# Loading the input in four quarters and spreading its transposes over the first three steps of a 1-core transformer kernel

## What is computed

```python
def rmsnorm(x, g, eps=NORM_EPS):
    xf = x.astype(jnp.float32)
    y = xf * lax.rsqrt(jnp.mean(xf * xf, axis=-1, keepdims=True) + eps)
    return (y * g.astype(jnp.float32)).astype(x.dtype)

for l in range(DEPTH):                 # DEPTH = 2
    h = rmsnorm(x, norm_g[l])
    proj = h @ w_in[l]                 # (256 x 1024) @ (1024 x 4096)
    ...                                # attention on parts of proj, gates
    x = x + y @ w_out[l]
```

## Time and profile before

| what | value |
|---|---|
| runs | 1212.27, 1209.83, 1209.98 us; median 1209.98 |
| the profiled execution's own time | 1208.38 us |
| its span | 1206.5 us |
| PE busy | 1187.9 us (98%) |
| DVE busy | 800.3 us (66%) |
| ACT busy | 586.7 us (49%) |
| POOL busy | 556.9 us (46%) |
| loaded | 297.92 MB, 247 GB/s in the mean |
| mean granted clock of PE | 0.999 |

### The profile page before, as it was taken

How to read it: one execution, slowest core, us unless ns; L and a number is a source line. 1 busy time by engine, 2 the same in 40 slices (tenths; PEclk the granted TensorE clock), 3 DMA queues, 4 the chain that set the end, 5 groups by cost and what they waited for, 6 DMA issues and landing times.

```text
span 1206.5 us, 15432 instructions
## 1 busy us (share of the span) xinstructions
PE 1187.9 (98%) x5752; PEld 975.4 (81%) x5752; DVE 800.3 (66%) x1118; ACT 586.7 (49%) x764; POOL 556.9 (46%) x418
## 2 busy tenths in 40 slices
PE   9999999999899999899999999999999999999998
PEld 6888887887688888788888888888888887888887
DVE  6885468844687688578768666697683675644423
ACT  5566465665543443444434357444352665534440
POOL 1466334564544343555454226764452462445460
PEclk9999999999999999999999999999999999999999
DMA  9976369845698899549988748799884444866550
GB/s 355 356 273 227 108 244 333 287 146 184 215 344 287 304 337 349 168 155 339 302 301 315 279 174 273 250 327 303 303 297 165 150 154 157 261 211 208 209 193 35
DMA packets 183224, 297.92 MB, mean 247 GB/s; under 512 B 8368, under 2 KB 100208, under 8 KB 183152
## 3 DMA queue, kind: packets, MB, share of 16 engines
q1 hardware_dynamic: 177696, 284.82, 68.2%
q10 hardware_dynamic: 5456, 12.13, 2.9%
HBM read 295.84 MB, written 1.08 MB: 246 GB/s over the span
## 4 chain that ended last, share of the span: by engine, by line
PE 88%; DVE 5%; POOL 2%; ACT 2%; issue 1%; SPq 1%; DMA 1%; ACTq 0%; DVEq 0%
PE ps L1821 26%; PE ps L1834 26%; PE ps L1826 25%; PE ps L2087 2%; PE ps L1848 1%; POOL w_lo L510 1%; PE ps L1971 1%; PE ps L1913 1%; PE ps L1999 1%; ACT w_hi L640 1%; DVE w_lo L1157 1%; PE ps L1987 1%; DMA raw<-w_in 1%; SPq L468 1%; PE ps L1959 1%
## 5 line engine op out<-in xcount | busy, mean ns | idle before, releaser
L510 POOL TENSOR_TENSOR w_lo<-raw,w_hi 128x512 fp32r<-128x512 f32 x348 | 479.5, 1411 | 447.0 <-ACT w_hi L640 447.0
L640 ACT ACTIVATE w_hi<-raw 128x2048 fp32r<-128x2048 f32 x188 | 354.6, 1910 | 102.9 <-PE ps L1834 68.8
L1821 PE MATMUL ps<-w_hi,h_hi 128*128 128x512 f32 x1120 | 313.8, 402 | 1.0 <-issue 1.0
L1834 PE MATMUL ps<-w_lo,h_hi 128*128 128x512 f32 x1120 | 301.4, 391 | 2.7 <-POOL w_lo L521 0.8
L1826 PE MATMUL ps<-w_hi,h_lo 128*128 128x512 f32 x1120 | 300.6, 390 | 0.0
L1157 DVE TENSOR_TENSOR w_lo<-raw,w_hi 128x2048 fp32r<-128x2048 f32 x96 | 224.9, 2346 | 111.4 <-ACT w_hi L640 108.6
L1834 PEld LDWEIGHTS ps<-w_lo,h_hi 128*128 128x128 f32 x1120 | 209.3, 188 | 50.1 <-issue 2.1
L1826 PEld LDWEIGHTS ps<-w_hi,h_lo 128*128 128x128 f32 x1120 | 210.1, 188 | 46.2 <-DVE h_lo L1218 0.2
L1821 PEld LDWEIGHTS ps<-w_hi,h_hi 128*128 128x128 f32 x1120 | 200.6, 188 | 43.7 <-issue 6.9
L1143 DVE SCALAR_TENSOR_TENSOR ps<-ada_raw,ccol,ps 128x512 f32<-128x512 f32 x240 | 181.0, 754 | 8.7 <-DMA ada_raw<-ada_w 2.0
L913 ACT ACTIVATE a_hi<-ps 128x512 fp32r<-128x512 f32 x44 | 26.3, 599 | 160.6 <-PE ps L2087 160.6
(11 more groups left out here) (198 smaller groups left out, 981.2 us busy)
## 6 DMA issues: line engine op xcount, KB each, us to landing
raw<-ffn_in SPq DMA_DIRECT2D x176, 512.0 KB, 5.7
ada_raw<-ada_w SPq DMA_DIRECT2D x144, 512.0 KB, 7.2
raw<-ffn_out SPq DMA_DIRECT2D x44, 1024.0 KB, 6.5
raw<-w_in SPq DMA_DIRECT2D x31, 1024.0 KB, 8.6
raw<-w_out SPq DMA_DIRECT2D x8, 1024.0 KB, 6.4
ada_raw<-kv_ada_w SPq DMA_DIRECT2D x16, 512.0 KB, 8.5
raw<-w_kv SPq DMA_DIRECT2D x8, 1024.0 KB, 6.0
bias<-na_bias ACTq DMA_DIRECT2D x16, 256.0 KB, 4.2
```

Source lines behind the costliest of these rows:

```text
L510: ins = pool.tensor_tensor(w_lo[:, u % RAW, piece], raw[:, u % RAW, piece], w_hi[:, u % RING, piece].bitcast(F32), ALU.subtract)
L640: act.activation(w_hi[:, u % RING, :], raw[:, u % RAW, :], ACT.Copy).then_inc(*S.inc("w_hi_ready", u))
L1821: pe.matmul(bank(b), hi[:, k_in_lhs + k, tok], wh[:, k, c * 512:(c + 1) * 512], start=start and k == 0, stop=False)
L1834: ins = pe.matmul(bank(b), hi[:, k_in_lhs + k, tok], wl[:, k, c * 512:(c + 1) * 512], start=False, stop=stop and k == nk - 1)
```

## The change

x is loaded in four quarters (token block by column half, 256 KB each), each with a semaphore of its own. On SP the order is x(0,0), first half of unit 0, x(1,0), second half of unit 0, x(0,1), x(1,1), unit 1. PE does two `warm_up` matmuls at the start instead of three, turns x(0,0) alone, and turns the other three quarters one by one in the middle of steps 0, 1 and 2: x(1,0), x(0,1), x(1,1). In the steps of unit 0 the matmuls on `w_hi` go by halves of the unit: `h_hi` and `h_lo` with its first two row blocks, then both with the other two. On ACT, `w_hi` of unit 1 stands between the `h_hi` of x(0,1) and that of x(1,1). DVE's order is the same as before.

```diff
-WARM_UP = (3, 1)
+WARM_UP = (2, 1)
...
-            sp.dma_start(x[:, 0, :], x_in[0:P, :]).then_inc(x_in_sem[0], 16)
+            def load_x(t, half):
+                cols = slice(512 * half, 512 * half + 512)
+                sp.dma_start(x[:, t, cols], x_in[t * P:(t + 1) * P, cols]).then_inc(x_in_sem[t][half], 16)
+
+            load_x(0, 0)
...
                             raw_in[0] if k else half_in, 16)
+                        if k == 0:
+                            load_x(1, 0)
...
                 if u == 0:
-                    sp.dma_start(x[:, 1, :], x_in[P:2 * P, :]).then_inc(x_in_sem[1], 16)
+                    load_x(0, 1)
+                    load_x(1, 1)
...
                 for t in range(NT):
+                    if t:
+                        fill(1)
                     act.wait_ge(*S.at("xT_done", "a0", t, 1))
...
                     ins.then_inc(*S.inc("h_hi_ready", "a0", t, 1))
-                fill(1)
                 act.wait_ge(*S.at("stat_filled"))
...
-                for k in range(nk):
-                    if u == 0 and k == nk // 2:
+                for part in (range(0, nk // 2), range(nk // 2, nk)) if u == 0 else (range(nk),):
+                    if u == 0 and part[0]:
                         pe.wait_ge(*S.at("w_hi_ready", 0))
-                    for c, b in enumerate(banks):
-                        pe.matmul(bank(b), hi[:, k_in_lhs + k, tok], wh[:, k, c * 512:(c + 1) * 512],
-                                  start=start and k == 0, stop=False)
-                lhs_wait(lo_ready)
-                for k in range(nk):
-                    for c, b in enumerate(banks):
-                        pe.matmul(bank(b), lo[:, k_in_lhs + k, tok], wh[:, k, c * 512:(c + 1) * 512],
-                                  start=False, stop=False)
+                    for k in part:
+                        for c, b in enumerate(banks):
+                            pe.matmul(bank(b), hi[:, k_in_lhs + k, tok], wh[:, k, c * 512:(c + 1) * 512],
+                                      start=start and k == 0, stop=False)
+                    lhs_wait(lo_ready)
+                    for k in part:
+                        for c, b in enumerate(banks):
+                            pe.matmul(bank(b), lo[:, k_in_lhs + k, tok], wh[:, k, c * 512:(c + 1) * 512],
+                                      start=False, stop=False)
                 between()
...
+            def raw_T(t, half):
+                pe.wait_ge(x_in_sem[t][half], 16)
+                transpose_half("a0", t, half, "xT_done")
...
                 if layer == 0:
-                    norm_T(name, 0)
+                    raw_T(0, 0)
                     warm_up(WARM_UP[1])
...
                 def between(s):
-                    if s == 0 and not layer:
-                        norm_T(name, 1)
+                    if s < 3 and not layer:
+                        raw_T(*((1, 0), (0, 1), (1, 1))[s])
```

More of the change, by code:

```diff
@@ L335, in program @@
         bias_in = [ctx.enter_context(nc.semaphore(f"bias_in{i}")) for i in range(BIASES)]
-        x_in_sem = [ctx.enter_context(nc.semaphore(f"x_loaded{t}")) for t in range(NT)]
+        x_in_sem = [[ctx.enter_context(nc.semaphore(f"x_loaded{t}_{half}")) for half in range(2)] for t in range(NT)]
         ROWS = {("down", 0, 0): 2, "pool": 5, "pool_scale": 4, "pool_shift": 3, ("down", 0, 1): 8,
@@ L806, in first_norm @@
                     ins.then_inc(*S.inc("h_hi_ready", "a0", t, 1))
-                fill(1)
                 act.wait_ge(*S.at("stat_filled"))
                 for t in range(NT):
-                    act.wait_ge(x_in_sem[t], 16)
+                    for half in range(2):
+                        act.wait_ge(x_in_sem[t][half], 16)
                     act.activation(hn[:, t, :], x[:, t, :], ACT.Square, accum_out=st(t)).then_inc(
@@ L1916, in norm_T @@
             def norm_T(name, t, hat=None):
-                if name == "a0":
-                    pe.wait_ge(x_in_sem[t], 16)
                 for half in range(2):
-                    transpose_half(name, t, half, "xT_done", [("x_hat_ready", hat or name, t)] if name != "a0" else ())
+                    transpose_half(name, t, half, "xT_done", [("x_hat_ready", hat or name, t)])
+            def raw_T(t, half):
+                pe.wait_ge(x_in_sem[t][half], 16)
+                transpose_half("a0", t, half, "xT_done")
             def mix_part(half, to, of):
```

## The result

| | before | after |
|---|---|---|
| median of the runs | 1210.99 us (4 runs, 1209.83 to 1212.27) | 1221.16 us (4 runs, 1220.42 to 1224.92) |
| ratio, 95% interval | | 1.009 [1.0065, 1.0114] |
| the profiled execution: time, span | 1208.38, 1206.5 us | 1224.92, 1222.8 us |
| its mean granted clock | 0.999 | 0.991 |

The changed kernel is slower by 0.9%, 10.2 us. The forecast was 1218.4 us, a loss of 8.4. The profiled execution of the changed kernel is the slowest of its four (the others took 1220.4 to 1221.4 us, at a clock of 0.994 to 0.996), so its trace shows more loss than the median: its span is 16.3 us longer than that of the kernel before.

A forecast was written before the change was run, and what follows sets the result against it. PE's own list was taken to set the end (busy 1187.9 of 1206.5 us). Stalls 7.2 - 0.2 given back + 1.4 for the clock = 8.4 us, on 1210.0 giving 1218.4 us; range 1214.5 to 1221.5 us.

The forecast's parts named there:

- The mechanism: Step 2: PE waits 2.1 us for ACT's `w_hi` of unit 1, then 4.7 us for DVE's `w_lo` of unit 1.
- Rival C: Step 2: only the first wait comes, as DVE makes `w_lo` of unit 1 ahead of x(1,1); 1212.1 us, chance 0.03.
- rival D: Not slower: loads go on during the stalls and PE catches up; 1210.0 or 1209.1 us, chance 0.05.
- rival A: Both waits of step 2 come but the clock stays high; loss 7.0 us, 1217.0 us, chance 0.18.
- rival B: Later PE waits, up to 300 us, swallow part of the loss; 4.8 to 6.2 us left, about 1215.5 us, chance 0.09.
- the clock: one fall, for 1.4 us: Step 2: PE comes out of the 4.7 us wait at 1.2 GHz, losing 1.4 us, the middle of 0 and 2.65.
- bound of 2.65 us: Upper bound of the clock loss behind step 2's second wait, from some 5.3 us of half-pace work at the start.
- the 7.2 us of the stalls: Step 2's `w_lo` matmuls start at 24.5 us instead of 17.33, a loss of 7.2 us.
- Cost 0: Start: loading x in quarters costs 0, with the second half of unit 0 landing at 7.9 us as before.
- The upper bound of 0.8 us: Loads at the start: most the quarters could cost if two more DMA issues delayed unit 0's second half, 0.8 us.
- `w_lo` of step 0 done at 10.6 us: Step 0: DVE, free at about 9.0 us, finishes `w_lo` in 1.57 us, so the `w_lo` matmuls start at 10.6.

The follow-up runs named there:

- e1: The changed kernel with ACT making `w_hi` of unit 1 ahead of both `h_hi` groups; 1217.94 us, ratio 1.0065 to the kernel before.
- e2: The changed kernel with DVE making `w_lo` of unit 1 between the `h_lo` of x(0,1) and that of x(1,1); 1218.53 us, ratio 1.0068.
- e6: The changed kernel with the loads of the kernel before (two blocks of 512 KB, the second behind unit 0); 1220.53 us, ratio 1.0087.
- e4: The changed kernel with matmuls on zeros where PE waits, two ahead of step 2 and five ahead of its `w_lo` matmuls; 1219.16 us, ratio 1.0072.
- e3: The changed kernel with the edits of e1 and e2 together; 1215.45 us, ratio 1.0043.
- e5: The kernel before with each x block loaded in two halves cut by columns (128 rows of 2 KB), in the old queue places; 1210.80 us, ratio 1.0006.
- e8: The kernel before with seven identity matmuls ahead of the first feed-forward layer's transposes of token block 0, while the wait is block 1's; 1209.22 us, ratio 0.9995.
- e10: The kernel before with each x block loaded in two pieces cut by partitions (64 rows of 4 KB), in the old queue places; 1212.95 us, ratio 1.0021.
- e11: e3 with the loads of the kernel before; 1213.75 us, ratio 1.003.
- e7: The changed kernel with unit 0 right behind x(0,0), the other three quarters turned in step 0, matmuls by halves in step 0 only; 1211.06 us, ratio 1.0011.
- e9: The kernel before with seven identity matmuls ahead of the first feed-forward layer's transposes of token block 1, where PE waits; 1208.77 us, ratio 0.9987.

## Where the prediction was right, and which step failed

*The mechanism was right, and all of it at the place named.* Two waits in step 2, for ACT's `w_hi` and DVE's `w_lo` of unit 1, because each stood in its engine's list behind work on a quarter of x that was now turned later: forecast 2.1 and 4.7 us, measured 2.25 and 4.59. e1 and e2 take away one each and leave the other unchanged, e6 shows that the loads are not in it. Rival C (only the first wait) and rival D (not slower) are out; rival A (the clock stays high) is out for the traced execution of the changed kernel. What A would have looked like is the traced execution of e4, without a fall: 8.4 us over the traced execution of the kernel before, against A's 7.0.

*No loss was given back* (rival B). The transposes at 328 us are still 12.75 us late, after 13.0 at step 4; the 0.2 us between them are about the wait of the earlier trace rows, which is gone, as forecast. PE's waits from 30 to 300 us are the same four rows as in the earlier trace rows with 2.1 us in all.

*The step that failed is the clock: one fall, for 1.4 us.* The runs showed two falls instead, one behind each wait, for 1.4 and 2.7 us by the comparison with e4, 4.1 us in all. That is above the prediction's own bound of 2.65 us. Two things were wrong in it. The sum had no fall behind the first wait, and the row that spoke for a high clock after such a wait was the 2.3 us at 509 us, with the clock at 1.00. One execution without a fall does not show that there is none: behind that same wait of 2.27 us the clock fell in 5 of the 13 traced executions (the changed kernel, e1, e2, e3, e5), and behind the wait for the first feed-forward layer, 1.9 to 2.0 us, in 7 of the 12 that have it. The wait of 2.25 us in step 2 itself is followed by a fall in the changed kernel and e6, and by none in e2. And the fall behind the second wait was put at the middle of 0 and 2.65 us, with no row for the middle; 2.65, from the slow stretch at the start, was almost what it cost (2.7). That stretch moves from run to run, though: the same six passes took 5.49 us in the kernel before, 4.64 in e5 and 4.45 in e8, with the same code up to there. The rule of the Trainium skill ("TensorE: Matmul & The Clock Gate", section "HAM oscillation — how this bites in real kernels"), by which PE starts slow after a wait between blocks, agrees with the changed kernel behind both waits, and not with e2.

*The second term that was too small:* the 7.2 us of the stalls. Without falls it is 8.4 us (e4: the `w_lo` matmuls of step 2 at 25.78 us, against 24.5 forecast and 17.33 before). The waits were right, but step 2 began 1.3 us late in e4, because steps 0 and 1 took longer than worked out. "Cost 0" for the quarters as transfers was wrong about the landing: the second half of unit 0 was to land when it did, since the bytes ahead of it are the same; it came at 9.1 us instead of 7.9 (8.7 to 8.9 in e1 to e4), and e5 and e10 get the same from nothing but smaller pieces. The upper bound of 0.8 us held only for some of these executions. But what it cost is 0.4 us (e6 at step 2), and the bigger error lies beside it: the forecast had `w_lo` of step 0 done at 10.6 us with DVE's 1.57 us. It was done at 11.43 in the changed kernel because the load was late, and at 11.43 in e6 with the load in time, because DVE took 2.37 us beside POOL. In the medians e6 is no more than 0.6 us under the changed kernel, with overlapping intervals.

The late landing is the point at which the Trainium skill ("DMA: Bandwidth & Descriptors", section "Measured (HBM→SBUF, 128 partitions, SWDGE, issued from GpSimd)") had warned against the change, and I set it aside because a queue full of 512 KB pieces ran at over 390 GB/s. The row was about 512 KB pieces; the window of e5 shows what pieces of 256 KB do at the start: 234 GB/s between 5 and 6 us, against 391 before.

*That the number came close is partly luck.* Against the median 8.4 us were forecast and 10.2 measured; the median lies within the range, near its upper end, and the traced execution, 1224.92 us, lies above it. But at step 4 the changed kernel is 13.0 us late, not 8.4. The medians are closer together because the executions of the kernel before carry losses of their own: its median of 1210.99 us is 2.6 us above its traced execution, which has no fall before its last matmul. Fastest against fastest over all comparisons it is 1208.34 and 1220.42 us, 12.1 us apart.

Two sums of the prediction do not come out. The lower end of the range is called B with A's clock; that is 4.8 us and would give 1213.2 us, not 1214.5. And C and D have chances of 0.03 and 0.05, but "faster" and "within it" together only 0.06.

What is left open is how the late falls are shared among executions of the changed kernel, since only one of four has a trace, and why smaller pieces of x bring the load behind them late.

## What to carry to other kernels

When a producer's result is moved later, look on every engine at what stands behind its consumer in that engine's list: here the loss came from `w_hi` and `w_lo` of unit 1, which did not depend on the moved transposes at all. An engine that goes without a pause before the consumer (DVE from 11.9 to 19.7 us) turns a later arrival into lateness of what follows: 2.8 us at `w_lo` of unit 1 in e11. An earlier first instruction on PE did not help it (e7: 1.5 us earlier at the start, 0.9 us later at step 2). A wait of PE costs its length and then, in some executions, a slow stretch as well, so one trace without a fall is no evidence that a wait is safe; cheap matmuls on constants in the wait take away the second part.

## What the runs showed of the hardware that was not expected

- The clock fell behind waits of 1.9 to 2.3 us in some executions and not in others: with the same wait of 2.04 us at the same place it fell in the changed kernel and not in the one before; with the same wait of 2.25 us it fell in the changed kernel and not in e2; with the same wait of 2.27 us it fell in 5 of 13 traces.
- With two loads of 256 KB in place of one of 512 KB ahead of unit 0 (and the same behind it), with the same bytes and order, the second half of unit 0 landed 1.2 us later when x was cut by columns (e5) and 1.4 us later when it was cut by partitions (e10).
- DVE's `w_lo` of 128x1024 took 1.23 us alone and 2.37 us where POOL's `w_lo` ran beside it for 1.3 us (e6; the same in e11); in e5, e8 and e9 it was POOL's pair that grew, from 2.5 to 3.5 or 3.6 us.
- Seven matmuls of the 128x128 identity, 14 passes in 1.72 us, kept the clock up through a wait in the traced execution, and the 11 runs lay within 1.3 us, where 23 of the kernel before lay within 3.9 (e9).
